# Attention scores as three products of rounded parts, with a ring of four gate buffers

## The reference, cut to what matters

```python
def block_attention(q, k, v):                 # 16 query heads, 4 key heads, head_dim 64
    def one_block(qi):                        # 128 queries
        s = jnp.einsum("bqkgd,bskd->bkgqs", qi, k).astype(jnp.float32) * scale
        p = jax.nn.softmax(s, axis=-1).astype(v.dtype)
        return jnp.einsum("bkgqs,bskd->bqkgd", p, v)

if ctx is None:                               # prompt tokens: 128 keys
    k_all, v_all = ak, av
else:                                         # latent tokens: 512 own keys and 128 cached ones
    aq = axial_rope(aq)
    k_all = jnp.concatenate([axial_rope(ak), ctx[0].astype(ak.dtype)], axis=1)
    v_all = jnp.concatenate([av, ctx[1].astype(av.dtype)], axis=1)
ha = block_attention(aq, k_all, v_all).reshape(B, T, A_WIDTH)
g = jax.nn.sigmoid(bg.reshape(B, T, 2, D_MODEL))
y = g[:, :, 0] * (hm.astype(h.dtype) @ w_bm) + g[:, :, 1] * (ha @ w_ba)
```

## Time and profile before

| | |
|---|---|
| median of three runs | 1703.99 us (1702.3, 1704.13, 1703.99) |
| profiled execution | 1704.33 us, span 1702.6 us |
| PE busy | 1679.4 us, 99% of the span |
| PE weight loads | 1545.3 us, 91% |
| DVE busy | 1044.2 us, 61% |
| ACT busy | 745.3 us, 44% |
| granted clock of PE | above 90% of full speed in all 40 slices, mean 0.997 |
| DMA | 189.66 MB, 111 GB/s |
| chain that ended last | PE 89%, DVE 4%, ACT 3% |

### The profile page before, as it was taken

The page is one execution under the profiler, slowest core; times in us unless marked ns, Lnnn a source line. Parts: engine busy times, 40 slices in busy tenths (PEclk is TensorE's granted clock), DMA queues, the critical chain, the costliest instruction groups (busy, mean ns, idle before and its releaser), DMA issues.

```text
span 1702.6 us, 27823 instructions
## 1 busy us (share of the span) xinstructions
PE 1679.4 (99%) x11327; PEld 1545.3 (91%) x11327; DVE 1044.2 (61%) x1779; ACT 745.3 (44%) x1402; POOL 0.2 (0%) x4
## 2 busy tenths in 40 slices
PE   8999999999999999999999999999999999999998
PEld 6998899989889888999999888889889989998997
DVE  5777687548666224555537877775646834872775
ACT  6312255325574332443445554553564433551452
POOL 0000000000000000000000000000000000000000
PEclk9999999999999999999999999999999999999999
DMA  9787222322613215233243211111621221332233
GB/s 386 279 319 262 75 66 84 100 61 89 210 54 111 84 62 113 82 95 87 81 149 118 67 52 42 42 41 58 228 87 50 75 87 62 100 97 77 74 105 144
DMA packets 56790, 189.66 MB, mean 111 GB/s; under 512 B 7464, under 2 KB 16472, under 8 KB 53848
## 3 DMA queue, kind: packets, MB, share of 16 engines
q1 hardware_dynamic: 56664, 187.89, 33.1%
HBM read 170.67 MB, written 16.54 MB: 110 GB/s over the span
## 4 chain that ended last, share of the span: by engine, by line
PE 89%; DVE 4%; ACT 3%; issue 1%; DMA 0%; DVEq 0%; ACTq 0%
PE psum L762 9%; PE psum L764 9%; PE psum L763 9%; PE psum L744 7%; PE psum L745 7%; PE psum L746 7%; PE psum L872 4%; PE psum L873 4%; PE psum L874 4%; PE psum L1288 2%; PE psum L1270 2%; PE psum L834 2%; PE psum L836 2%; PE psum L835 2%; PE psum L1248 2%; PE psum L1173 1%
## 5 line engine op out<-in xcount | busy, mean ns | idle before, releaser
L1906 DVE TENSOR_TENSOR wlo<-raw,whi 128x1024 fp32r<-128x1024 f32 x120 | 146.8, 1224 | 310.4 <-ACT whi L1382 310.3
L1382 ACT CAST whi<-raw 128x1024 fp32r<-128x1024 f32 x120 | 125.5, 1046 | 257.2 <-PE psum L874 125.1
L762 PE MATMUL psum<-g_hi,whi 128*128 128x320 f32 x656 | 209.4, 319 | 0.2 <-ACT gate L1724 0.2
L764 PE MATMUL psum<-g_hi,wlo 128*128 128x320 f32 x656 | 202.7, 309 | 0.0
L763 PE MATMUL psum<-g_lo,whi 128*128 128x320 f32 x656 | 202.6, 309 | 0.0
L762 PEld LDWEIGHTS psum<-g_hi,whi 128*128 128x128 f32 x656 | 123.2, 188 | 4.9 <-issue 1.9
L872 PE MATMUL psum<-whi,g_hi 128*128 128x512 f32 x320 | 125.0, 390 | 0.0
L874 PE MATMUL psum<-whi,g_lo 128*128 128x512 f32 x320 | 124.5, 389 | 0.0
L873 PE MATMUL psum<-wlo,g_hi 128*128 128x512 f32 x320 | 124.5, 389 | 0.0
L763 PEld LDWEIGHTS psum<-g_lo,whi 128*128 128x128 f32 x656 | 123.3, 188 | 0.7
L764 PEld LDWEIGHTS psum<-g_hi,wlo 128*128 128x128 f32 x656 | 123.1, 188 | 0.0
(11 more groups left out here) (446 smaller groups left out, 4386.2 us busy)
## 6 DMA issues: line engine op xcount, KB each, us to landing
raw<-in_w_ffn_in SPq DMA_DIRECT2D x88, 512.0 KB, 3.6
raw<-in_w_mix SPq DMA_DIRECT2D x77, 512.0 KB, 4.1
raw<-in_w_ffn_out SPq DMA_DIRECT2D x44, 512.0 KB, 3.6
direct<-in_w_mod SPq DMA_DIRECT2D x7, 2048.0 KB, 9.4
mw<-in_w_mod SPq DMA_DIRECT2D x14, 768.0 KB, 5.4
mw<-in_w_mod SPq DMA_DIRECT2D x8, 1024.0 KB, 16.8
gate<-gate_keep SPq DMA_DIRECT2D x24, 320.0 KB, 5.2
gate_keep<-gate SPq DMA_DIRECT2D x20, 320.0 KB, 4.6
```

The lines of the kernel that those rows point to most:

```text
L762: mm(out, wh[:, k, :], hi[:, k, cols], start=(k == 0), stop=False)
L764: last = mm(out, wl[:, k, :], hi[:, k, cols], start=False, stop=(k == nk - 1))
L1382: copy((to or whi[t.slot])[:, :, :], raw[t.raw][:, :, :]).then_inc(w_hi, 1)
L1906: tt(lo[:, :, :], raw[t.raw][:, :, :], hi[:, :, :].bitcast(F32), ALU.subtract).then_inc(raw_free, 1)
```

## The change

The scores of the latent pairs become products of rounded parts, as the large products are. The keys (four tiles: two and their swapped copies, each 128x640) and the queries (128x512 for each of eight tiles, the latent columns) are split: the high parts by ACT (key_high, query_high), the low parts by DVE in place (key_low, query_low). For each head three products of 64 rows and 320 columns are added up, twice, for the two halves of the 640 keys. The scores of the two prompt pairs stay as they are, and read a copy of the prompt's keys (akp). The cached keys take the place of the prompt's keys in the first 128 columns of ak, once these are stored and copied; the scores of a head begin at column 192 of its bank pair (KEY_AT), and the values follow the new order of the keys. The high key parts lie in the four upper gate buffers, so the gates from 8 on use a ring of the four lower ones. fill(0) moves ahead of scores(0). The query parts 0 and 1 are made before the loop, the others two pairs ahead, in the loop.

```diff
             def take_kept(i):
+                slot = i if i < KC else i % RING
                 if i >= KC:
-                    sp.wait_ge(gate_used, i - KC + 1)
-                sp.dma_start(gate[i % KC][:, :], a["gate_keep"][i]).then_inc(gate_in[i % KC], 16)
+                    sp.wait_ge(gate_used, i - (KC if i < KC + RING else RING) + 1)
+                sp.dma_start(gate[slot][:, :], a["gate_keep"][i]).then_inc(gate_in[slot], 16)
 
...
-                    if 0 <= l - 6 - L_BM < KC:
-                        take_kept(2 * KC + l - 6 - L_BM)
+                    if 0 <= l - 6 - L_BM < 2 * KC - RING:
+                        take_kept(KC + RING + l - 6 - L_BM)
...
             for hh in range(2):
                 sp.dma_start(ak[hh * HD:(hh + 1) * HD, NKC:2 * NKC, :],
                              ak[(1 - hh) * HD:(2 - hh) * HD, 0:NKC, :]).then_inc(ak_sw, 16)
+                sp.dma_start(akp[hh * HD:(hh + 1) * HD, NKC:2 * NKC, :],
+                             ak[(1 - hh) * HD:(2 - hh) * HD, 0:NKC, 0:TP]).then_inc(ak_sw, 16)
+            sp.dma_start(akp[:, 0:NKC, :], ak[:, 0:NKC, 0:TP]).then_inc(ak_sw, 16)
             sp.dma_start(a["o_k"].rearrange("p (n t) -> p n t", n=NKC), ak[:, 0:NKC, 0:TP]).then_inc(misc_st, 16)
-            mix(L_AQ + 6, L_BM + 2)
+            mix(L_AQ + 6, L_AQ + 8)
+            sp.wait_ge(ak_sw, 80)
+            sp.wait_ge(misc_st, 16 * 6)
+            sp.dma_start(ak[:, :, 0:PAST], a["cache_k"].rearrange("p (n s) -> p n s", s=PAST)).then_inc(ck_in, 16)
+            mix(L_AQ + 8, L_BM + 2)
...
-            for i in range(KC, 2 * KC):
+            for i in range(KC, KC + RING):
...
@@ -1228,10 +1249,9 @@
                 if k >= 1:
                     pe.wait_ge(aexp, 2 * k)
                 else:
-                    pe.wait_ge(ck_in, 32)
-                    pe.wait_ge(ak_sw, 32)
+                    pe.wait_ge(ak_sw, 80)
                 if k < KC:
-                    pe.wait_ge(rope_out, NKC + m + 1)
+                    pe.wait_ge(qk_lo, KC + 2 * NKC + m + 1)
...
                             last = mm(psum[:, 2 * s, j * P:(j + 1) * P], aq[half[s], 4 * m + j, 0:TP],
-                                      ak[half[s], key, 0:TP], start=True, stop=True)
+                                      akp[half[s], key, :], start=True, stop=True)
...
-                    for b in range(2):
-                        for s in range(2):
-                            mm(psum[:, 2 * s, 2 * b * P:2 * (b + 1) * P], aq[half[s], m, c * P:(c + 1) * P],
-                               ak[half[s], key[s], TP + 2 * b * P:TP + 2 * (b + 1) * P], start=True, stop=True)
-                    for s in range(2):
-                        last = mm(psum[:, 2 * s + 1, 0:PAST], aq[half[s], m, c * P:(c + 1) * P],
-                                  akc[half[s], g, :], start=True, stop=True)
+                    tok = slice(c * P, (c + 1) * P)
+                    for h in range(2):
+                        for n, (q, kk) in enumerate(((q_hi, k_hi), (q_hi, k_lo), (q_lo, k_hi))):
+                            for s in range(2):
+                                out = flat(s)[:, KEY_AT + h * HALF:KEY_AT + (h + 1) * HALF]
+                                last = mm(out, q[half[s], m, tok], kk[half[s], key[s], HCOLS[h]], start=(n == 0), stop=(n == 2))
                 last.then_inc(sc, 1)
...
-                                      av[:, b + 1, (m // 2) * HD:(m // 2 + 1) * HD], sbb[:, s, b * P:(b + 1) * P],
+                                      av[:, b or NT, (m // 2) * HD:(m // 2 + 1) * HD], sbb[:, s, b * P:(b + 1) * P],
...
+            fill(0)
             scores(0)
             qk_stats(QK - 1)
-            fill(0)
             fill(1)
...
+            def key_high(n):
+                if n == 0:
+                    act.wait_ge(ak_sw, 80)
+                    act.wait_ge(ck_in, 32)
+                    act.wait_ge(gate_used, KC)
+                copy(k_hi[:, n, :], ak[:, n, :]).then_inc(qk_hi, 1)
+
+            def query_high(m):
+                act.wait_ge(rope_out, NKC + m + 1)
+                copy(q_hi[:, m, TP:N], aq[:, m, TP:N]).then_inc(qk_hi, 1)
+
             for l in range(L_AV, L_BM):
                 t = Tile(T_MIX + l)
                 done(t)
+                if l == L_BM - 1:
+                    query_high(0)
...
+                if l == L_BM - 2:
+                    for n in range(2 * NKC):
+                        key_high(n)
...
-                    last = fn(sa[s][:, :], flat(s)[:, 0:N], ACT.Exp, bias=amax[:, s:s + 1], accum_out=asum[:, s:s + 1])
+                    last = fn(sa[s][:, :], flat(s)[:, KEY_AT:KEY_AT + N], ACT.Exp, bias=amax[:, s:s + 1], accum_out=asum[:, s:s + 1])
...
             def gate_of(i):
-                act.wait_ge(gate_in[i % KC], 16 * (i // KC + 1))
-                fn(gate[i % KC][:, :], gate[i % KC][:, :], ACT.Tanh, scale=0.5).then_inc(gate_sg, 1)
...
+                gate_ready(act, i)
+                fn(gate_of_slot(i)[:, :], gate_of_slot(i)[:, :], ACT.Tanh, scale=0.5).then_inc(gate_sg, 1)
...
+            query_high(1)
             inv_rms(QK - 1)
             exponentials(0, 0)
             exponentials(0, 1)
             act.preload_act_table_set("exp_and_others")
             for k in range(PAIRS):
+                if k + 2 < KC:
+                    query_high(k + 2)
                 take_p(k)
...
+            def key_low(n):
+                dve.wait_ge(qk_hi, KC + n + 1)
+                tt(k_lo[:, n, :], ak[:, n, :], k_hi[:, n, :].bitcast(F32), ALU.subtract).then_inc(qk_lo, 1)
+
+            def query_low(m):
+                dve.wait_ge(qk_hi, KC + 2 * NKC + m + 1)
+                tt(q_lo[:, m, TP:N], aq[:, m, TP:N], q_hi[:, m, TP:N].bitcast(F32), ALU.subtract).then_inc(qk_lo, 1)
+
+            for n in range(2 * NKC):
+                key_low(n)
 
...
-                    dve.tensor_reduce(amax[:, s:s + 1], flat(s)[:, 0:N], AX.X, ALU.max, negate=True).then_inc(nmx, 1)
+                    dve.tensor_reduce(amax[:, s:s + 1], flat(s)[:, KEY_AT:KEY_AT + N], AX.X, ALU.max, negate=True).then_inc(nmx, 1)
...
+            query_low(0)
+            query_low(1)
             top(0, 0)
             top(0, 1)
...
+                if k + 2 < KC:
+                    query_low(k + 2)
                 divide(k)
```

More of the change, by code:

```diff
@@ L73 @@
 ROW_TILES = (6, 8, 6)
+KEY_AT = 512 - HALF
 TURNED = ((0, 1), (2, 3), (0, 1), (1, 3), (5, 7))
@@ L286, in build @@
         ak = place("ak", [P, 2 * NKC, N])
-        akc = place("akc", [P, KVH, PAST])
+        akp = place("akp", [P, 2 * NKC, TP])
         av = place("av", [P, NT + 1, KVH * HD])
@@ L302, in build @@
         m_lo = at("m_lo", [P, KC, N], F32R, h_at + KC * row)
+        k_hi = at("k_hi", [P, 2 * NKC, N], F32R, x_at + 4 * row)
+        k_lo = at("k_lo", [P, 2 * NKC, N], F32R, mw_at)
+        q_hi, q_lo = m_hi, m_lo
         assert max(end_m, end_a, tail_at + MOD_W * 4) <= nc.sbuf_usable_end
@@ L414, in values_out, with gate_of_slot, gate_ready @@
             return psum[:, MV_BANKS[f][c], :]
+        def gate_of_slot(i):
+            return gate[i if i < KC else i % RING]
+        def gate_ready(engine, i):
+            if i < KC:
+                engine.wait_ge(gate_in[i], 16)
+            else:
+                engine.wait_ge(gate_in[i % RING], 16 * ((i - KC) // RING + 2))
         def kept(i):
@@ L434, in build @@
         dve_sums, tok_sum, tok_hi, tok_lo = mod0_in[0:4]
-        mod0_mm, mod0_copy, mod0_t, ld_cst = sem("mod0_mm"), sem("mod0_copy"), sem("mod0_t"), sem("ld_cst")
+        mod0_mm, mod0_copy, mod0_t, ld_cst = sem("mod0_mm_then_qk_hi"), sem("mod0_copy_then_qk_lo"), sem("mod0_t"), sem("ld_cst")
+        qk_hi, qk_lo = mod0_mm, mod0_copy
         cols_in = sem("cols_in")
@@ L682, in _ @@
             sp.wait_ge(misc_st, 16 * 5)
-            sp.dma_start(akc[:, :, :].rearrange("p g s -> p (g s)"), a["cache_k"]).then_inc(ck_in, 16)
             sp.dma_start(av[:, NT, :], a["cache_v"]).then_inc(ck_in, 16)
@@ L2698, in take_a @@
                 dve.wait_ge(ba_done, m + 1)
-                stt(sq[0][:, HALF:N], gate[m][:, HALF:N], 1.0, psum[:, FILL_BANK, 0:HALF],
+                stt(sq[0][:, HALF:N], gate_of_slot(2 * KC + m)[:, HALF:N], 1.0, psum[:, FILL_BANK, 0:HALF],
                     ALU.add, ALU.mult).then_inc(ba_ev, 1)
@@ L2711, in take_fill @@
                 cols = slice(h * HALF, (h + 1) * HALF)
-                stt(yg[:, m, cols], gate[m][:, cols], 1.0, psum[:, FILL_BANK, 0:HALF],
+                stt(yg[:, m, cols], gate_of_slot(KC + m)[:, cols], 1.0, psum[:, FILL_BANK, 0:HALF],
                     ALU.add, ALU.mult).then_inc(ev[t.slot] if h else half_ev, 1)
@@ L2753, in _ @@
                 m = (l - L_BM) % KC
-                g = gate[m]
+                g = gate_of_slot(2 * KC + m)
                 if L_BA < l < L_OUT - 2:
@@ L2851, in lay_out @@
         "m0": f("state_m")[0, 0].T, "state_C": f("state_C"), "state_n": f("state_n"),
```

(3 more changed lines are left out.)

## The result

| | before | after |
|---|---|---|
| median of ten runs each | 1704.46 us (1702.3 to 1707.53) | 1709.33 us (1707.68 to 1711.28) |
| profiled execution, span | 1704.33, 1702.6 us | 1711.28, 1709.4 us |
| PE, DVE, ACT busy | 1679.4, 1044.2, 745.3 us | 1675.6, 1052.3, 754.0 us |
| granted clock of PE, mean | 0.997 | 0.995 |

The ratio is 1.0032, with a 95% interval of 1.0023 to 1.004: the change costs 4.9 us, where 0.7 was forecast. PE is busy for 3.8 us less and the kernel takes longer, so PE waits more.

A forecast was written before the change was run, and what follows sets the result against it. PE, 99% busy, was taken to bound the kernel, with DVE second. Cheaper scores -4.4, query parts 0.0 and the start +5.05 made +0.7 us, so 1704.7 us on the median's scale; range 1699 to 1710.

The forecast's parts named there:

- rival B: At the start, PE's clock falls in the new gap; about +3.5 us on first transposes, 1708.2 us; chance 0.15.
- term 3: Loops 0 to 5: query rounding on ACT and subtraction on DVE eat up the shorter scores; 34.1 against 34.06, 0.0 us.
- Scores on PE: Score block of 32 of 34 pairs takes 1.09 us against 1.29, row halves side by side; 0.20 saved a loop.
- A: Score blocks on PE have no edges at switches, loop 5.23 us; total -4.6 us, 1699.4 us; chance 0.20.
- C: Score row halves don't run side by side on PE, 1.97 us a pair; about +25, 1730 us; chance with worse 0.10.
- Which loops keep it: Loops 6 to 21 and 26 to 31, 22 bound by PE, keep the scores' saving: -4.4 us.
- The start: Four key subtractions and the first query's on DVE stand ahead of scores(0) and delay what follows: +5.05 us.
- SP queue: Three more copy issues and the moved load of cached keys are lost in waits for raw buffers: no cost.
- Gate ring: Gate i waits for gate i-4, each wait met before the next weight load's raw buffer comes free: no cost.
- Order of the values: Value products in the new key order and scores at KEY_AT: same counts and sizes, no effect.

The follow-up runs named there:

- e3: Changed kernel with the query parts made three pairs ahead in the loop instead of two; median 1706.46 us, ratio 1.0017 to the kernel before.
- e5: Changed kernel with constant filler products in both PE gaps of the start, eight before scores(0), three before scores(1); 1707.44 us, ratio 1.0021.
- e1: Changed kernel with eight constant filler products between fill(0) and scores(0), nothing else; 1707.82 us, ratio 1.0023.
- e2: Changed kernel with PE's order fill(0), statistics of query 7, fill(1), scores(0); 1710.21 us, ratio 1.0031.
- e8: e6 with the subtractions of queries 6 and 7 in passes 9 and 11 instead of 8 and 9; 1700.75 us, ratio 0.9988.
- e6: Changed kernel with latent pairs ordered by halves of the query tiles, fewer subtractions ahead of scores(0), the others in later passes; 1703.89 us, ratio 0.9992.
- e7: e6 with four constant filler products ahead of scores(0) and three behind scores(1); 1701.87 us, ratio 0.9983.
- e9: e7 with the subtractions of queries 6 and 7 in passes 9 and 11; 1702.33 us, ratio 0.999.
- e4: Kernel before with only the ring of four gate buffers for the gates from 8 on; 1704.11 us, ratio 1.0004.

## Why the prediction went as it did

The time lies inside the range given, but the forecast's case, no measurable difference, did not come: it is slower by more than 0.2%, for a sum of terms of which one was wrong and one too small. There is luck in the range: 1709.33 is 0.7 below its upper end, that end had room for rival B, and the larger of the two errors, term 3, has no rival of its own in the prediction.

1. *Scores on PE.* Right. 1.07 against 1.09 forecast; the row halves work side by side with rounded operands, at the step of the full-array row. A (no edges) and C (one after the other) are out.
2. *Which loops keep it.* Right: 22 loops at 5.42 to 5.44, -4.6 for -4.4; loops 22 to 25 kept their times to 0.03, bound as before.
3. *Query parts in loops 0 to 5.* This step failed, by 3.0 of the 4.2 us that the sum was off. It priced query_low as a delay of the division alone: "loops 0, 3, 4 and 5 have room for it before the values end". For the division that is so. But scores(k+2) of pass k+1 stand right behind the values of pass k on PE and wait for this very subtraction; PE is free for them 1.24 behind the start of the values (1022.74 - 1021.50 in the earlier trace rows); in loop 0 the subtraction started 1.02 behind it and took 0.69, and the scores came 1.86 behind it, at 979.63, 0.62 late (the row's bracket counts 0.54 of that as waiting). Forecast 5.49, 6.49, 5.81, three of 5.44; measured 6.04, 7.11, 6.49, 6.03, 5.43, 5.99. Five of six are 0.55 to 0.68 over, about the subtraction's own 0.61, now on PE's path; only loop 4 is as forecast: its pass has neither a weight subtraction nor an eviction ahead of the query's, which started 0.33 behind the values. e3 took the wait away and got 33.64.
4. *The start.* The way to scores(0) was right: rel 8.19 measured, and 8.1 forecast (965.6 - 957.49), gap 3.98 for 3.9. Behind it, the forecast took the full clock, and so gave +5.05; e5, with the clock held up, has +5.16. The changed kernel itself had a fallen clock there, and that is rival B, given 0.15: the fall came where it was said, and its size was wrong. I had priced it at 3.5; from scores(0) to the first transposes it cost 16.40 - 15.11 = 1.3, because the clock was back when fill(1) and scores(1) ran, and only the way from scores(0) over the statistics to ACT's logarithm was slow. Why it falls stays open. The rule beside rival B (the Trainium skill, TensorE: Matmul & The Clock Gate, "Why this matters for your kernels"), that idle gaps between bursts cost speed, agrees with after, with its gap of 3.98. In the starts of the profiled executions the clock fell in five of the six without both gaps filled (after, e1, e2, e3, e8; not e6) and in none of the three with both filled (e5, e7, e9). But e6 and e8 have the same gap to 0.01 us at scores(0) (1.76 and 1.75) and differ, and before fell at 592 without a gap. The prediction's argument that "the granted clock of the page doesn't fall anywhere" read too coarse a view: before's trace has the falls at 456 and 592, the first behind a gap of 1.77 only, and they speak for B.
5. *SP queue.* No cost, as forecast: the cached keys were asked for at 915.35 and first needed by ACT at 954.67, no wait of the stage names a transfer, and the steady loops are PE's own.
6. *Gate ring.* No cost: e4.
7. *Order of the values.* Nothing seen.

So of +4.89, the start is +6.48 (5.2 what stands ahead of the first scores, 1.3 the clock, by the difference of after and e5), the late query parts +3.0, and the cheaper products give back 4.6.

## What to carry to other kernels

When a preparation moves into a loop, ask of each of its results who reads it next and how soon, not only what it pushes back on its own engine: a 0.6 us subtraction with room for it cost 0.6 a pass because the next instruction on PE waited for it, and nothing when it was made one pass sooner. Work that must come before the first pass of a pipeline is paid in full, so order the passes such that few prepared parts are needed at the start (e6 to e9: the same arithmetic, a stage 7 us shorter than after's and 2 shorter than before's).

Before arguing from the clock row of a page, ask how long a slice is: 40 slices of 43 us hid two falls of about 4 us. And when the effect is some us in 1700, compare the stage in traces, loop by loop, beside the medians.

## What the runs showed of the hardware that I had not expected

- The granted clock falls to the lower level in the middle of a kernel that is 98% busy, and not in every execution. In the start it did so behind a gap of 4 us or less, for about 3 us (after: 0.50 in 967.5 to 969), up to 6 (e2: 972 to 978). In before it did so at 456, behind a wait of 1.77, and at 592, behind 2.8 us of very small products without a gap; e4, with the same instructions there, fell at neither. In e1, with one gap of the start filled, the fall came later; what decides it, no run here shows.
- Products of rounded operands with 64 rows, one in each row half, run two at a time at 0.147 a pair of 320 columns, as fast as one full-array product of that width.
